# Four tiles in place of two in the first pass over h

## The chip, the cores and the metric

One core of a Trainium2 chip runs the whole kernel in one launch. The metric is the time of the device in microseconds (us), lower is better. Matrix products run on TensorE (PE in the profile), everything elementwise on VectorE (DVE) and ScalarE (ACT), a few small steps on GpSimd (POOL), and SyncE (SP) issues the loads of weights.

## The reference, cut to what matters

Two transformer blocks follow each other on a sequence of 256 tokens with 2048 channels, all in float32. The part of the first block that the change touches:

```python
h = rms_norm(x, mix_norm_g)
q, kv, gate_logits, conv_in = split(h @ w_in)     # conv_in: 2 x 1024 columns
conv = silu(layer_norm(causal_depthwise_conv(a * sigmoid(gate))))   # a, gate = halves of conv_in
attn = nsa_attention(q, kv, gates, ...)           # compressed, selected and window branches
x = x + concat([attn, conv]) @ w_out
h = rms_norm(x, ffn_norm_g)
u = causal_depthwise_conv(h @ w_up, 3 taps)       # 2 x 5632 columns
x = x + (silu(gate) * a) @ w_down                 # a, gate = halves of u
```

The second block (adaptive scales from `c`, latent attention, gated linear attention, a gated feed-forward) takes the result.

## The kernel before, in words

**Precision.** Every large product is made of three: both operands are split into a high part (float32r) and the rest, and high x high, rest x high and high x rest are added in PSUM. For the weights ScalarE rounds a chunk (`w_hi`, L1147) and VectorE subtracts (`w_lo`, L1623).

**Weights.** All weights come in one stream of 933 chunks of 128 x 1024, in an order written by `make_plan`: 737 to be split, 4 raw ones and 192 of `w_ada`, which VectorE multiplies with silu(c) and sums (L1605) in between, at a rate per split chunk that `ada_until` sets. SyncE loads up to seven chunks ahead into `raw`; a slot is free again when its rest is taken. ScalarE and VectorE split up to four ahead (`PART_SLOTS`); `lead(i)` is the third split chunk behind chunk i, and both engines split that far before they take the result of the tile that ends with chunk i.

**Tiles and groups.** A tile is 128 output columns of a projection, with the weights as the stationary operand: 16 steps k over the 2048 channels, two chunks. Its result is [128 columns, 256 tokens] in one PSUM bank. Up-projection tiles use `h_both`, high and rest of h side by side, 512 columns (L593, L594); the others take three matmuls of 256 columns (L596 to L598). A group is 512 output columns with h (or the mixed values) stationary, two banks, one for each 128 tokens (L603, L606). `tiles["of"]` is the rotation of banks that tiles go through, (4, 5, 2, 3), `tiles["turn"]` the place in it; groups name their two banks. The rotation is set anew at L875 (behind the attention), at L1013 and at L1092. `free[b]` is the semaphore that says when bank b has been read, and `fill(b)` waits for it before the first matmul of a tile or a group.

**h stages.** Four times (stages 0 to 3) a normed x in `wide` is turned by TensorE (two transposes per k, L671, banks 6, 7, 0, 1), rounded by ScalarE (`h_hi`, L1179) and its rest taken by VectorE (`h_lo`, L1677). `need(k)` in `h_need` turns up to three k ahead of the k that the matmuls take. Stages 0 and 1 come before the convolution's projections and before the first feed-forward; there the first pass is a pair of tiles by turns (`tile_pair`), so that each k feeds two tiles. `WITH_H` says at which k ScalarE and VectorE put a weight chunk between.

**Order behind it.** After the pair of stage 0: a small matmul of the table of position biases (L702), the other 14 convolution tiles, 4 tiles for the compression, its small layer, 8 query tiles, one of gates, 4 key tiles, the group `value` in banks 2 and 7, then the attention's 16 units with the convolution's output projection between their steps. The last key tile is read by ScalarE (L1250), behind the silus of the convolution (L1260); the first scores need it. After the pair of stage 1, for each half of the feed-forward: its up tiles (44 in all, 22 for the value and 22 for the gate, those of the pair among them in half 0), each joined by VectorE (L1910), then the down-projection in four groups of banks (0, 1), (2, 3), (0, 1), (2, 3), each added to x by VectorE (L1878). Then the second block begins: stage 2, `c_q` in banks (0, 1), `c_kv` in (2, 3), four `gla_q` and four `gla_k` tiles (read by ScalarE, L1406), with turned latents in banks 0 and 1 and 6 and 7 between them, and the group `gla_v` 0 in (0, 1).

Of the kernel before, what the change touches and what calls it, by code (L numbers as in the profile page):

```python
# [13 lines left out]
P = 128  # L14
T = 256
TT = T // P
D = 2048
KD = D // P
# [11 lines left out]
DFF = 5632  # L30
# [36 lines left out]
class Plan:  # L67
# [3 lines left out]
    def __init__(self):  # L71
        self.chunks = []
        self.kinds = []
        self.groups = {}
        self.pairs = {}
        self.ada = [(v, kt, half) for v in range(6) for kt in range(KD) for half in range(2)]
        self.rate = 0.0
        self.due = 0.0
        self.keep = 0
        self.on_pool = set()  # L80
        self.pool_rate = 0.0
        self.pool_due = 0.0
        self.open = False
# [29 lines left out]
    def project(self, key, mat, col, n, k0=0, nk=KD, order=None):  # L113
        self.groups[key] = [self.piece(mat, kt, col, n) for kt in order or range(k0, k0 + nk)]

    def project_pair(self, key, first, second, mat, cols, n):
        self.groups[key] = [self.piece(mat, kt, col, n) for kt in range(KD) for col in cols]
        self.pairs[first] = self.pairs[second] = key

    def raw(self, key, mat, pieces):  # L120
        self.groups[key] = []
# [11 lines left out]
            self.put_ada()  # L133


def make_plan():
    p = Plan()
    kv = HEADS * DH
    gates = kv + N_BRANCH * 512
    conv = gates + N_BRANCH * HEADS  # L140
    p.project_pair("conv_first", ("conv_a", 0), ("conv_g", 0), "w_in", (conv, conv + CONV_CH), P)
    for j in range(1, CONV_TILES):
        p.project(("conv_a", j), "w_in", conv + P * j, P)
        p.project(("conv_g", j), "w_in", conv + CONV_CH + P * j, P)
    for s in range(2):
        for j in range(2):
            p.project(("cmp", s, j), "w_in", kv + 256 * s + P * j, P)
    p.raw("cmp_w1", "cmp_w1", 2 * CMP_LEN * DH // CHUNK)
    for j in range(8):
        p.project(("query", j), "w_in", P * j, P)  # L150
    p.project("gates", "w_in", gates, N_BRANCH * HEADS)
    for br in (1, 2):
        for j in range(2):
            p.project(("key", br, j), "w_in", kv + 512 * br + P * j, P)
    p.project("value", "w_in_v", 0, 512)
    for n in range(4):
        p.project(("out_conv", n), "w_out", 512 * n, 512, KD // 2, KD // 2)
    for n in range(4):
        p.ada_until(2 * KD, 0.58 if n in (1, 2) else 0)
        p.project(("out_attn", n), "w_out", 512 * n, 512, 0, KD // 2)  # L160
    for half in range(2):
        if half == 0:
            p.project_pair("up_first", ("up_a", 0), ("up_g", 0), "w_up", (0, DFF), P)
        p.ada_until(2 * KD, 0.53)
        for j in range(FF_HALF * half or 1, FF_HALF * (half + 1)):
            p.project(("up_a", j), "w_up", P * j, P)
            p.project(("up_g", j), "w_up", DFF + P * j, P)
        p.ada_until(2 * KD, 0.76)
        for n in range(4):
            p.project(("down1", half, n), "w_down", 512 * n, 512, FF_HALF * half, FF_HALF)  # L170
    p.finish_ada()
    p.project("c_q", "w_in_2", 0, Q_RANK)
    p.project("c_kv", "w_in_2_kv", 0, KV_RANK + ROPE + GATE_RANK)
    at = Q_RANK + KV_RANK + ROPE
    for h in range(GLA_HEADS):
        p.project(("gla_q", h), "w_in_2", at + P * h, P)
    at += GLA_HEADS * GLA_K
    for h in range(GLA_HEADS):
        p.project(("gla_k", h), "w_in_2", at + P * h, P)
    at += GLA_HEADS * GLA_K  # L180
    for n in range(2):
        p.project(("gla_v", n), "w_in_2", at + 512 * n, 512)
    at += GLA_HEADS * GLA_V + GATE_RANK
    for n in range(2):
        p.project(("gla_r", n), "w_in_2", at + 512 * n, 512)
    p.project("q_rope", "w_uq_rope", 0, MLA_HEADS * ROPE, 0, Q_RANK // P)
    for h in range(MLA_HEADS):
        p.project(("q_nope", h), "w_uq_nope", P * h, P, 0, Q_RANK // P)
    for h in range(MLA_HEADS):
        p.project(("k_nope", h), "w_uk", P * h, P, 0, KV_RANK // P)  # L190
    for n in range(2):
        p.project(("mla_v", n), "w_uv", 512 * n, 512, 0, KV_RANK // P)
    for n in range(4):
        p.project(("out2", n), "w_out_2", 512 * n, 512, order=MIX_ORDER)
    p.open = False
    p.ada_until(0, 0.2)
    for half in range(2):
        for g, col, n in FF_GROUPS[half]:
            p.project(("gate", g), "w_ffn_gate", col, n)
            p.project(("up", g), "w_ffn_up", col, n)  # L200
        for n in range(4):
            p.project(("down2", half, n), "w_ffn_down", 512 * n, 512, FF_HALF * half, FF_HALF)
    return p
# [36 lines left out]
class Stream:  # L240


    def __init__(self, plan):
# [19 lines left out]
        for key, pieces in plan.groups.items():  # L263
# [8 lines left out]
                        self.used[i] = n  # L272
            self.done[key] = n
            self.final[key] = pieces[-1][0]
        for key, pair in plan.pairs.items():
            self.done[key], self.final[key] = self.done[pair], self.final[pair]


class Seen:
# [11 lines left out]
def two_blocks(nc, WEIGHTS, X, PARAMS, PARAMS1, PARAMS2, POSITIONS, COND, FINAL_ROW, OUT):  # L291
# [12 lines left out]
    with ctx:  # L304
# [163 lines left out]
        banks = [both[:, 0, :], both[:, 1, :]] + [ctx.enter_context(nc.psum_tensor(f"bank{b}", [P, 512], F32)) for b in range(2, 8)]  # L468
        bank_of = {}
        FIRST_CHUNKS = (0, groups["up_first"][0][0], c_first, gate_first)  # L470
        WITH_PAIR = {0: 0, 2: 1, 4: 2, 6: 3, 11: 4}
        WITH_GROUP = {k: k // 2 for k in range(0, KD, 2)}
        WITH_H = (WITH_PAIR, WITH_PAIR, WITH_GROUP, WITH_GROUP)
        TURN_BANKS = ((6, 7, 0, 1), (6, 7, 0, 1), (6, 7, 4, 5), (6, 7, 4, 5))
        LATENT_BANKS = (6, 7, 0, 1, 6, 7)
        WITH_GLA_Q = ((), (), (), (0, 1))
# [86 lines left out]
        def tensor_program(e):  # L563
# [121 lines left out]

                return need

            def tile_pair(key, first, second, a_hi, a_lo, need, free_first, free_second, a_both=None):
                both = (4, 5)
                tiles["turn"] += 2  # L690
                bank_of[first], bank_of[second] = both
                whole(project(key, P, both, [banks[b][:, 0:T] if a_both is None else banks[b][:, :] for b in both], a_hi, a_lo, need, True, by_turns=True, a_both=a_both))
                free[4], free[5] = free_first, free_second

            w.wait_ge(gains_landed, 16)
            need = h_need(0, lambda k: (h_ready, k + 1))
            tile_pair("conv_first", ("conv_a", 0), ("conv_g", 0), h_hi, h_lo, need, (conv_a_ready, 1), (conv_g_ready, 1))
            K1 = BUCKETS + 1
            w.wait_ge(params_landed, 16)
            w.wait_ge(params1_landed, 16)  # L700
            fill(7)
            e.matmul(banks[7][0:HEADS, 0:ROW], param1("rel_bias")[0:K1, :], param1("one_hot")[0:K1, :], start=True, stop=True).then_inc(table_made, 1)  # L702
            free[7] = table_ready, 1
            for j in range(1, CONV_TILES):
                tile(("conv_a", j), h_hi, h_lo, need, (conv_a_ready, j + 1))
                tile(("conv_g", j), h_hi, h_lo, need, (conv_g_ready, j + 1))
            for s in range(2):
# [171 lines left out]
                free[pair[0]], free[pair[1]] = (residual, 8 + 2 * n + 1), (residual, 8 + 2 * n + 2)  # L879

            need = h_need(1, lambda k: (h_ready, 16 + k + 1))
            tile_pair("up_first", ("up_a", 0), ("up_g", 0), h_hi, h_lo, need, (up_joined, 1), (up_joined, 2), h_both)
            for half in range(2):
                for j in range(FF_HALF * half or 1, FF_HALF * (half + 1)):
                    wide_tile(("up_a", j), need, (up_joined, 2 * j + 1))
                    wide_tile(("up_g", j), need, (up_joined, 2 * j + 2))
                ff_need = lambda k, half=half: w.wait_ge(ff_ready, FF_HALF * half + k + 1)
# [1743 lines left out]
```

## Time and profile before

| | us |
|---|---|
| three timed runs | 2235.58, 2238.95, 2239.26 |
| their median | 2238.95 |
| the profiled execution | 2235.5 |
| its span, first to last instruction | 2233.7 |
| TensorE busy | 2193.6 |
| VectorE busy | 1611.1 |
| ScalarE busy | 1119.3 |

A row of the timeline gives the start and the length of an instruction, or of a run of like ones (x8), and in square brackets the idle time ahead of it with what ended it. Matmuls overlap: one of 512 columns shows about 0.39 us, while the next starts 0.23 us after it, so the starts tell the pace and a short wait doesn't show as idle time. A row of the windows gives, for a stretch, its length, the busy time of each engine with the number of instructions, the granted TensorE clock as a share of the full one, the busy share of the DMA engines and GB/s.

### The profile page before, as it was taken

The numbers are of one execution on the slowest core, as the hardware profiler recorded it, in microseconds if no ns is written. First come the engines' busy times: TensorE is split into PE (matmuls) and PEld (weight loads), VectorE is DVE, ScalarE is ACT, GpSimd is POOL, SyncE is SP. The second block draws the span as 40 slices with busy tenths as digits, with TensorE's granted clock in tenths as the row PEclk, the third lists the DMA queues.
The fourth block names the chain that finished last, engine by engine and source line by source line (L and its number), as shares of the span: only waits on it lengthen the run. The fifth ranks groups of instructions, "written<-read, shape, count | busy, mean of one in ns | idle before, by whom it ended". The sixth has DMA issues, their size and how long they took to land.

```text
span 2233.7 us, 30478 instructions
## 1 busy us (share of the span) xinstructions
PE 2193.6 (98%) x12130; PEld 1883.6 (84%) x12130; DVE 1611.1 (72%) x2423; ACT 1119.3 (50%) x1670; POOL 29.6 (1%) x63
## 2 busy tenths in 40 slices
PE   7999999999999999999989999989999999999998
PEld 7999887888888888888879787878888888888986
DVE  6998885899998799998865655566555555544555
ACT  5434774555554455554454655555444444444343
POOL 1000000000000000000000000000000000000000
PEclk9999999999999999999999999999999999999999
DMA  8644436688889888889955551647666677655563
GB/s 271 217 162 142 153 97 209 221 294 285 291 301 369 320 281 289 291 287 361 341 157 185 179 179 57 225 134 250 226 228 224 227 230 232 217 188 190 187 211 120
DMA packets 138223, 504.13 MB, mean 226 GB/s; under 512 B 15616, under 2 KB 15760, under 8 KB 137184
## 3 DMA queue, kind: packets, MB, share of 16 engines
q1 hardware_dynamic: 136512, 494.42, 65.5%
q0 software_dynamic: 1280, 5.65, 1.0%
q8 instruction: 96, 1.57, 0.3%
q10 hardware_dynamic: 288, 2.10, 0.3%
q14 instruction: 47, 0.39, 0.0%
HBM read 499.61 MB, written 2.51 MB: 225 GB/s over the span
## 4 chain that ended last, share of the span: by engine, by line
PE 85%; DVE 11%; ACT 2%; issue 1%; DMA 0%; POOL 0%; SPq 0%; DVEq 0%; ACTq 0%; POOLq 0%
PE bank L603 20%; PE both L603 18%; PE bank L606 10%; PE both L606 9%; PE bank L593 7%; DVE w_lo L1623 5%; PE bank L594 4%; PE bank L596 4%; PE bank L598 4%; PE bank L597 4%; DVE raw L1605 2%; ACT ffn_a L1345 1%; ACT ffn_g L1351 1%; PE bank L830 1%; PE both L787 1%
## 5 line engine op out<-in xcount | busy, mean ns | idle before, releaser
L1623 DVE TENSOR_TENSOR w_lo<-raw,w_hi 128x1024 fp32r<-128x1024 f32 x737 | 893.8, 1221 | 450.1 <-ACT w_hi L1147 448.6
L1147 ACT ACTIVATE w_hi<-raw 128x1024 fp32r<-128x1024 f32 x737 | 767.9, 1054 | 640.9 <-PE bank L606 296.6
L593 PE MATMUL bank<-h_both,w_hi 128*128 128x512 f32 x1408 | 356.5, 394 | 1.8 <-DVE h_both L1677 1.8
L593 PEld LDWEIGHTS bank<-h_both,w_hi 128*128 128x128 f32 x1408 | 253.2, 189 | 47.0 <-DVE h_both L1677 2.5
L1605 DVE SCALAR_TENSOR_TENSOR raw<-raw,silu_c 128x1024 f32<-128x1024 f32 x192 | 233.9, 1218 | 0.0
L603 PE MATMUL bank<-w_hi,h_both 128*128 128x512 f32 (+2 forms) x1024 | 233.9, 372 | 0.0
L603 PE MATMUL both<-w_hi,h_both 128*128 128x512 f32 (+1 forms) x960 | 231.9, 383 | 1.7 <-DVE h_both L1697 1.7
L603 PEld LDWEIGHTS bank<-w_hi,h_both 128*128 128x128 f32 x1024 | 181.8, 188 | 33.1 <-issue 0.3
L594 PEld LDWEIGHTS bank<-h_both,w_lo 128*128 128x128 f32 x1408 | 192.1, 190 | 13.7
L603 PEld LDWEIGHTS both<-w_hi,h_both 128*128 128x128 f32 x960 | 171.3, 191 | 34.5 <-DVE h_both L1697 2.9
L594 PE MATMUL bank<-h_both,w_lo 128*128 128x256 f32 x1408 | 196.3, 282 | 0.0
L596 PE MATMUL bank<-h_both,w_hi 128*128 128x256 f32 (+1 forms) x656 | 165.1, 288 | 0.6 <-DVE h_both L1677 0.6
L597 PE MATMUL bank<-h_both,w_hi 128*128 128x256 f32 (+1 forms) x656 | 162.5, 284 | 0.0
L596 PEld LDWEIGHTS bank<-h_both,w_hi 128*128 128x128 f32 (+1 forms) x656 | 125.6, 191 | 2.2 <-DVE h_both L1677 1.1
L606 PE MATMUL bank<-w_lo,h_both 128*128 128x512 f32 (+2 forms) x512 | 126.4, 371 | 0.0
L597 PEld LDWEIGHTS bank<-h_both,w_hi 128*128 128x128 f32 (+1 forms) x656 | 125.7, 192 | 0.1
L606 PE MATMUL both<-w_lo,h_both 128*128 128x512 f32 (+1 forms) x480 | 121.5, 377 | 0.0
L603 PE MATMUL bank<-w_hi,ff_hi 128*128 128x512 f32 x352 | 111.0, 389 | 0.0
L603 PE MATMUL bank<-w_hi,ff_lo 128*128 128x512 f32 x352 | 111.0, 389 | 0.0
L603 PE MATMUL both<-w_hi,ff_hi 128*128 128x512 f32 x352 | 108.7, 390 | 0.6 <-ACT w_hi L1147 0.6
L603 PE MATMUL both<-w_hi,ff_lo 128*128 128x512 f32 x352 | 108.5, 389 | 0.0
L606 PEld LDWEIGHTS bank<-w_lo,h_both 128*128 128x128 f32 x512 | 91.4, 188 | 16.2
(366 smaller groups left out, 2624.4 us busy)
## 6 DMA issues: line engine op xcount, KB each, us to landing
raw<-weights SPq DMA_DIRECT2D x924, 512.0 KB, 4.5
raw<-weights SPq DMA_DIRECT2D x5, 504.0 KB, 4.2
x<-x SPq DMA_DIRECT2D x2, 1024.0 KB, 5.6
bias<-bias_rows POOLq DMA_DIRECT2D x8, 256.0 KB, 11.6
silu_c<-c ACTq DMA_DIRECT2D x2, 1024.0 KB, 4.6
gate_row<-gate_rows POOLq DMA_DIRECT2D x2, 1024.0 KB, 8.7
out<-x SPq DMA_DIRECT2D x8, 256.0 KB, 2.1
final_row<-final_row POOLq DMA_DIRECT2D x1, 1024.0 KB, 5.1
```

Source lines behind the costliest of these rows:

```text
L593: return e.matmul(out, hi, a_both[:, k, :, :].rearrange("p a t -> p (a t)"), start=first, stop=last)
L594: return e.matmul(out[:, 0:T], lo, a_hi[:, k, :], start=False, stop=False)
L596: e.matmul(out, hi, a_hi[:, k, :], start=opens and first, stop=False)
L597: return e.matmul(out, hi, a_lo[:, k, :], start=False, stop=False)
L598: return e.matmul(out, lo, a_hi[:, k, :], start=False, stop=closes and last)
L603: t = e.matmul(outs[o], stationary[:, k, o * P:(o + 1) * P], hi, start=opens and first and stationary is a_hi, stop=False)
L606: t = e.matmul(outs[o], a_hi[:, k, o * P:(o + 1) * P], lo, start=False, stop=closes and last)
L787: t = e.matmul(both[:, side, br * n:(br + 1) * n], queries[r, j, tt * P:(tt + 1) * P], keys[r, br, j // GQA, 0:n], start=True, stop=True)
L830: t = e.matmul(banks[b][DH * side:DH * side + DH, 0:P], values[:, sb, br, hk * DH:(hk + 1) * DH], weights_T[v % 2][:, (2 * side + br) * (t ...
L1147: e.activation(w_hi[:, n % PART_SLOTS, 0:widths[i]], raw[:, i % RAW_SLOTS, 0:widths[i]], ACT.Copy).then_inc(hi_ready, 1)
L1605: e.scalar_tensor_tensor(src, src, 1.0, silu_c[:, half, :], ALU.mult, ALU.mult, accum_out=ada_parts[:, v, kt, half:half + 1]).then_inc(ada ...
L1623: e.tensor_tensor(w_lo[:, slot, 0:widths[i]], raw[:, i % RAW_SLOTS, 0:widths[i]], w_hi[:, slot, 0:widths[i]].bitcast(F32), ALU.subtract).t ...
```

## The change

In stages 0 and 1 the first pass takes four tiles by turns, two of each half of the projection, in place of two. The plan orders their weights as k by k of four tiles, eight chunks; `WITH_H` has the same places in all four stages. `tile_four` puts them in banks 4, 5, 2 and 3 and sets the rotation of the tiles behind it to six banks.

```diff
-    def project_pair(self, key, first, second, mat, cols, n):
+    def project_four(self, key, tiles, mat, cols, n):
         self.groups[key] = [self.piece(mat, kt, col, n) for kt in range(KD) for col in cols]
-        self.pairs[first] = self.pairs[second] = key
+        for of in tiles:
+            self.fours[of] = key
...
+FIRST_CONV = [("conv_a", 0), ("conv_g", 0), ("conv_a", 1), ("conv_g", 1)]
+FIRST_UP = [("up_a", 0), ("up_g", 0), ("up_a", 1), ("up_g", 1)]
...
-    p.project_pair("conv_first", ("conv_a", 0), ("conv_g", 0), "w_in", (conv, conv + CONV_CH), P)
-    for j in range(1, CONV_TILES):
+    p.project_four("conv_first", FIRST_CONV, "w_in", (conv, conv + CONV_CH, conv + P, conv + CONV_CH + P), P)
+    for j in range(2, CONV_TILES):
...
-            p.project_pair("up_first", ("up_a", 0), ("up_g", 0), "w_up", (0, DFF), P)
+            p.project_four("up_first", FIRST_UP, "w_up", (0, DFF, P, DFF + P), P)
         p.ada_until(2 * KD, 0.53)
-        for j in range(FF_HALF * half or 1, FF_HALF * (half + 1)):
+        for j in range(FF_HALF * half or 2, FF_HALF * (half + 1)):
...
-        WITH_PAIR = {0: 0, 2: 1, 4: 2, 6: 3, 11: 4}
-        WITH_GROUP = {k: k // 2 for k in range(0, KD, 2)}
-        WITH_H = (WITH_PAIR, WITH_PAIR, WITH_GROUP, WITH_GROUP)
+        WITH_H = ({k: k // 2 for k in range(0, KD, 2)},) * 4
...
-            def tile_pair(key, first, second, a_hi, a_lo, need, free_first, free_second, a_both=None):
-                both = (4, 5)
-                tiles["turn"] += 2
-                bank_of[first], bank_of[second] = both
-                whole(project(key, P, both, ..., by_turns=True, a_both=a_both))
-                free[4], free[5] = free_first, free_second
+            def tile_four(key, members, a_hi, a_lo, need, frees, a_both=None):
+                tiles["of"], tiles["turn"] = (4, 5, 2, 3, 0, 1), 4
+                four = tiles["of"][0:4]
+                for of, b in zip(members, four):
+                    bank_of[of] = b
+                whole(project(key, P, four, ..., by_turns=True, a_both=a_both))
+                for b, free_at in zip(four, frees):
+                    free[b] = free_at
```

The loops on TensorE behind both calls start at j = 2 in place of 1. ScalarE's and VectorE's programs change only through the plan and `WITH_H`.

## Rows read from the trace of the kernel before

**Rows 1.** The profile's first part: busy us, share, instructions of each engine.

```profile
PE 2193.6 (98%) x12130; PEld 1883.6 (84%) x12130; DVE 1611.1 (72%) x2423; ACT 1119.3 (50%) x1670; POOL 29.6 (1%) x63
```

**Rows 2.** Waits of TensorE, for h: us in total, times, longest.

```profile
PE bank L593 <- DVE h_both L1677: 1.8, 2, 1.3
PE bank L596 <- DVE h_both L1677: 0.6, 1, 0.6
```

**Rows 3.** Timeline of TensorE in the h stages: start, length, what.

```profile
16.27 0.63 PE L671 MATMUL bank<-lasting,wide 128*128 128x128 f32 x2
16.68 0.58 PE L596 MATMUL bank<-h_both,w_hi 128*128 128x256 f32 x1
...
400.73 0.38 PE L671 MATMUL bank<-lasting,wide 128*128 128x128 f32 x2
401.61 0.73 PE L593 MATMUL bank<-h_both,w_hi 128*128 128x512 f32 x2 [0.49 <-DVE h_both L1677]
...
404.49 0.38 PE L671 MATMUL bank<-lasting,wide 128*128 128x128 f32 x2
404.62 0.71 PE L593 MATMUL bank<-h_both,w_hi 128*128 128x512 f32 x2
```

**Rows 4.** Windows of both pairs, and of the two tiles behind the second.

```profile
13.97:30.46 16.49, 16.49 (x121) 16.12 (x121) 14.27 (x36) 11.17 (x20) 0.00 (x0) 1.00 0.72 281
...
394.27:410.51 16.24, 15.74 (x88) 13.20 (x89) 13.66 (x26) 9.23 (x17) 0.00 (x0) 0.90 0.54 161
410.51:421.65 11.14, 11.14 (x65) 9.83 (x64) 9.73 (x16) 4.92 (x9) 0.00 (x0) 1.00 0.69 221
```

**Rows 5.** Timeline of TensorE where value begins, and the second unit's scores.

```profile
233.14 2.00 PE L603 MATMUL bank<-w_hi,h_both 128*128 128x512 f32 x8
...
242.48 1.13 PE L787 MATMUL both<-keys,queries 64*128 64x256 f32 x8
```

**Rows 6.** Timeline of ScalarE there: the last rounding and the key's copy.

```profile
236.84 1.04 ACT L1147 ACTIVATE w_hi<-raw 128x1024 fp32r<-128x1024 f32 x1
237.79 0.36 ACT L1250 ACTIVATE keys<-bank 128x256 f32<-128x256 f32 x1
```

**Rows 7.** Idle ahead of two h stages (timeline), and TensorE's windows with granted clock.

```profile
391.94 0.55 PE L671 MATMUL bank<-lasting,wide 128*128 128x128 f32 x3 [3.05 <-DVE wide L1637]
...
1135.69 1.75 PE L671 MATMUL bank<-lasting,wide 128*128 128x128 f32 x7 [4.18 <-DVE wide L1637]
...
394.00:396.00 2.00, 1.73 (x5) 0.50 0.54 106
396.00:398.00 2.00, 2.00 (x9) 0.66 0.72 211
...
1143.00:1145.00 2.00, 2.00 (x8) 0.53 1.08 35
...
217.00:219.00 2.00, 0.48 (x4) 1.00 0.00 0
```

**Rows 8.** Timelines where half 1 of the up-projection begins: TensorE, VectorE.

```profile
765.75 1.98 PE L593 MATMUL bank<-h_both,w_hi 128*128 128x512 f32 x8
...
765.95 1.29 DVE L1878 TENSOR_TENSOR x<-bank,x 128x512 f32<-128x512 f32 x2 [0.34 <-PE bank L606]
```

**Rows 9.** Timelines where gla_v begins: TensorE, ScalarE.

```profile
1228.78 1.09 PE L603 MATMUL both<-w_hi,h_both 128*128 128x512 f32 x4
...
1231.14 0.69 PE L942 MATMUL bank<-a_lr,phase 16*128 16x256 f32 x2 [0.81 <-DVE a_lr L2093]
...
1228.98 0.39 ACT L1406 ACTIVATE gla_k<-bank 128x256 f32<-128x256 f32 x1
```

**Rows 10.** Timelines behind the pairs: VectorE's join, ScalarE's rounding, VectorE's later wait.

```profile
413.91 0.42 DVE L1910 TENSOR_TENSOR up_a<-bank,up_low 128x256 f32<-128x256 f32 x1
...
416.88 1.99 ACT L1147 ACTIVATE w_hi<-raw 128x1024 fp32r<-128x1024 f32 x2
...
135.18 0.76 DVE L1766 TENSOR_TENSOR tokens<-bank,phase 128x256 f32<-128x256 f32 x2 [1.37 <-PE bank L598]
```

More of the change, by code:

```diff
@@ L74, in __init__ @@
         self.groups = {}
-        self.pairs = {}
+        self.fours = {}
         self.ada = [(v, kt, half) for v in range(6) for kt in range(KD) for half in range(2)]
@@ L274, in __init__ @@
             self.final[key] = pieces[-1][0]
-        for key, pair in plan.pairs.items():
-            self.done[key], self.final[key] = self.done[pair], self.final[pair]
+        for key, four in plan.fours.items():
+            self.done[key], self.final[key] = self.done[four], self.final[four]
 class Seen:
@@ L686, in h_need @@
                 return need
-            def tile_pair(key, first, second, a_hi, a_lo, need, free_first, free_second, a_both=None):
-                both = (4, 5)
-                tiles["turn"] += 2
-                bank_of[first], bank_of[second] = both
-                whole(project(key, P, both, [banks[b][:, 0:T] if a_both is None else banks[b][:, :] for b in both], a_hi, a_lo, need, True, by_turns=True, a_both=a_both))
-                free[4], free[5] = free_first, free_second
+            def tile_four(key, members, a_hi, a_lo, need, frees, a_both=None):
[3 more added lines that the diff above has]
+                    bank_of[of] = b
+                whole(project(key, P, four, [banks[b][:, 0:T] if a_both is None else banks[b][:, :] for b in four], a_hi, a_lo, need, True, by_turns=True, a_both=a_both))
+                for b, free_at in zip(four, frees):
+                    free[b] = free_at
             w.wait_ge(gains_landed, 16)
             need = h_need(0, lambda k: (h_ready, k + 1))
-            tile_pair("conv_first", ("conv_a", 0), ("conv_g", 0), h_hi, h_lo, need, (conv_a_ready, 1), (conv_g_ready, 1))
+            tile_four("conv_first", FIRST_CONV, h_hi, h_lo, need, [(conv_a_ready, 1), (conv_g_ready, 1), (conv_a_ready, 2), (conv_g_ready, 2)])
             K1 = BUCKETS + 1
@@ L703, in tensor_program @@
             free[7] = table_ready, 1
-            for j in range(1, CONV_TILES):
+            for j in range(2, CONV_TILES):
                 tile(("conv_a", j), h_hi, h_lo, need, (conv_a_ready, j + 1))
@@ L881, in tensor_program @@
             need = h_need(1, lambda k: (h_ready, 16 + k + 1))
-            tile_pair("up_first", ("up_a", 0), ("up_g", 0), h_hi, h_lo, need, (up_joined, 1), (up_joined, 2), h_both)
+            tile_four("up_first", FIRST_UP, h_hi, h_lo, need, [(up_joined, i + 1) for i in range(4)], h_both)
             for half in range(2):
-                for j in range(FF_HALF * half or 1, FF_HALF * (half + 1)):
+                for j in range(FF_HALF * half or 2, FF_HALF * (half + 1)):
                     wide_tile(("up_a", j), need, (up_joined, 2 * j + 1))
```

## The prediction

> **What bounds the kernel now.** I read the busy table first: TensorE is busy for 2193.6 of the span of 2233.7 us, VectorE for 1611.1, ScalarE for 1119.3 [rows 1]. So a change pays only where TensorE stands still. The list of TensorE's waits comes second, because the change is made to shorten waits for h: in the two stages that it touches TensorE waited for `h_both` for 1.8 + 0.6 us in all, three times [rows 2]. Then the timeline of TensorE through the second of these stages, for waits too short to be listed [rows 3], and a table of its busy time there [rows 4]. After that I left the stages and followed the banks, since the diff also changes which PSUM bank every later tile takes; what decides lies there [rows 5 to 9].
>
> **The h stages: what four tiles can win.** TensorE turns h (two transposes per k) and multiplies each k as soon as VectorE has its low half. With a pair a k brings 2 tiles of work, with four it brings 4; matmuls, transposes and weight chunks are the same in number, only earlier or later in the order. In the feed-forward stage a pair of transposes takes 0.13 us until the next matmul starts (404.49 to 404.62), but at 400.73 it is 0.88, so 0.75 too much [rows 3]. At the half clock such a pair takes 0.28 elsewhere and 0.41 at 16.27 to 16.68 us [rows 3], 0.13 too much; two more such places, one in each stage, hold 0.20 together. The first matmul's own waits (0.57 and 1.34 us) stay: they end with h's first low half, which four tiles don't bring sooner. With four, one k lasts about 1.2 us of TensorE and VectorE needs per two k two low halves (0.40 each, start to start) and one chunk's rest (1.22), 2.0 against 2.9 or more, so nothing is late there. Gain: 0.75 + 0.13 + 0.20 = 1.1 us. Its ends: nothing, if the waits only move; and, at the other end, all that the stages take beyond plain matmuls. The pair takes 16.24 us where the next two tiles take 11.14, 5.1 more, and the convolution's pair 16.49, where its 96 matmuls of 0.12 us would take 11.5, so 5.0 more [rows 4]. Most of this is 12 to 16 pairs of transposes and the half clock, which stay.
>
> **The burst behind four tiles.** Four tiles end at once, and ScalarE must open all four before it rounds the fourth chunk ahead. From the first join to the rounding that follows two tiles took 413.91 to 416.88, 3.0 us [rows 10]; the second two also carry a product, a silu and a rounding, so I estimate 3.4 to 4.4 us more, with about 0.5 to begin. The three chunks ready give TensorE 3 x 2.79 = 8.4 us (11.14 us for four chunks [rows 4]). The fourth is then rounded at 7.4 to 8.4: 0 to 0.3 us late. I take 0.2, with 0 and 3 as ends, because VectorE is nearly full there (9.73 of 11.14 us [rows 4]) and may not catch up. In the convolution VectorE starts its taps some 2 us later, since the sigmoid's table and four openings now come together. That lag has until VectorE's wait of 1.37 us at 135.18 us [rows 10] to vanish, and the short waits of 0.22 us per 11.5 us before it: cost 0. The table of position biases is made some 12 us later, but its rows are read by VectorE only after all taps, past 200 us: cost 0. Two chunks of the ada stream move from the first up-projection to the end of the second down-projection, where VectorE waits for ScalarE between two chunks: cost 0.
>
> **The banks: where it loses.** Before, tiles rotate over (4, 5, 2, 3), groups of two banks over (0, 1) and (2, 3). `tile_four` sets the rotation to (4, 5, 2, 3, 0, 1) at turn 4, and it stays so until it is set again. Counting turns gives the bank of each tile that a group of another kind follows.
>
> Place A, the end of the keys. Turns: 4 + 12 convolution tiles + 4 + 8 + 1 = 29 for key (1, 0), so key (2, 1) has turn 32, 32 mod 6 = 2, bank 2 (before: 32 mod 4 = 0, bank 4). `value` follows at once, in banks 2 and 7, and `fill(2)` now waits for `keys_ready` 4, ScalarE's copy of that key. In the trace value starts at 233.14 [rows 5], right behind the key's last matmul. ScalarE copies the key only at 237.79 to 238.15, behind eight silus of the convolution and two roundings, the last of them at 236.84, none of which wait for `value` [rows 6]. Before, two steps of value, 5.6 us, hide this. Now TensorE stands from 233.3 to 238.15: 4.9 us. Nothing behind it takes it back but a hidden wait of about 0.3 us at 242.48, where the second unit's scores wait for VectorE [rows 5]: of the lines of TensorE's waits none lies between 239 and 388 us, so there it is the bound. Net 4.6. Queued behind the waiting matmul are value's eight steps, all 16 attention units and the projections; ScalarE's rounding of chunks 73 and 74 waits in turn, with time to spare. Ends: 3.5, if ScalarE and VectorE had run ahead afterwards by more than I see, and 5.1.
>
> The clock at A. After the idle of 3.05 and 1.34 us the granted clock was 0.50 from 394 and rose inside 396:398 [rows 7]; after 4.18 + 1.42 us it was 0.50 from before 1137 until past 1143 [rows 7]. These are the two levels of 1.2 and 2.4 GHz. A stands 4.9 us in one piece, between the two, so I expect a fall. Half speed for 3.1 us costs 1.6 us, for some 6 us 3.0. I take 2.1, and 0 and 3.0 as ends: 0 because the shorter idle of 217:219 (busy 0.48 of 2.00 us) left the clock at 1.00 [rows 7].
>
> The Trainium skill (TensorE: Matmul & The Clock Gate, What's actually happening) says that the gate follows how busy TensorE has lately been, by a beat that doesn't start with the kernel, so that the length of the slow stretch differs between runs. By it the 2.1 us would scatter over the same ends; no row of one run can show that.
>
> Place B, from the first down-projection back to up tiles. Half 0 has 40 tiles in turns 4 to 43; up_a 22 has turn 44, 44 mod 6 = 2, bank 2 (before: bank 4). The last down group sits in (2, 3) and its residual must be added first. Its last matmul's slot ends at 765.75, VectorE starts the two additions at 765.95, 1.29 us for both, so the first ends near 766.64 [rows 8]: 0.9 us of wait, with 0.7 and 1.2 as ends (a rest or an ada sum a little late). The second bank is free by then. Half 1 ends with turns 86 and 87 in banks 2 and 3, but its first down group takes (0, 1), free long before.
>
> Place C, the second block. gla_k 3 has turn 95, bank 1, and gla_v 0 in (0, 1) waits for its copy, 1228.98 to 1229.37 instead of starting at 1228.78: 0.65 us. But six matmuls later TensorE already waits 0.81 us, until 1231.14, for VectorE's `a_lr`, whose chain doesn't hang on gla_v [rows 9]. So C costs 0; without that cover, 0.65.
>
> In the trace the rotation over four banks never makes a tile wait: both waits of tiles are for h [rows 2]. So two more banks bring nothing, and the rotation now meets the groups' banks. Against this reading stands the Trainium skill (Perfetto Trace Analysis, Matmul Optimizations), which advises to use all eight PSUM banks. By it six banks cost nothing and A and B fall out of the sum, which is then -0.9.
>
> **Sum.** -1.1 + 0.2 + 4.6 + 2.1 + 0.9 = +6.7 us. The profiled execution took 2235.5 (span 2233.7 and 1.8 around it), so 2242.2 by it. The runs shown spread from 2235.58 to 2239.26 with the median at 2238.95; the mean of the four times is 2237.3, and with 6.7 that is 2244. By the median it would be 2245.7.
>
> **Rivals.**
> 1. The stall at A leaves the clock at full: 4.6 in place of 6.7, so +4.6, 2242. For it: the idle lies between two steady stretches of matmuls, while both falls shown come behind idle cut by transposes. Against it: 3.05 + 1.34 us was enough.
> 2. The other side: the h stages are a chain of waits and not of work. If doubling the matmuls per k hid the transposes and the half clock too, the gain would be up to 5.1 + 5.0 = 10.1 and the sum 6.7 + 1.1 - 10.1 = -2.3, so 2235, not slower. It decides from a gain of 6.7 us on. For it: the excess is there [rows 4]. Against it: TensorE's busy time fills 16.49 of 16.49 and 15.74 of 16.24 us [rows 4].
> 3. The change costs nothing at the banks: -1.1 + 0.2 = -0.9, 2236. It holds only if ScalarE had the key's copy done when value starts; the trace has it 4.65 us later [rows 5, 6]. (The rule of the Trainium skill named at C, Matmul Optimizations in Perfetto Trace Analysis, would give this.)
> 4. The burst: VectorE's lag behind the four up tiles doesn't vanish in the half, or the convolution's lag reaches the queries, where VectorE already sets the pace. Some 3 us more: +9.5, 2247.
>
> **Chances.** Forecast 0.6, rival 1 0.12, rival 2 0.07, rival 3 0.07, rival 4 0.14. A measurement tells 0.2%, 4.5 us, from no change. The forecast lies 2.2 us beyond that, and with its ends 4 of 5 of it count as slower; half of rival 1, all of rival 4: 0.48 + 0.06 + 0.14, about 0.7 slower. Rivals 2 and 3 are mostly within 0.2%: 0.26 same, 0.04 faster. The range goes from 2239 (gain 2, clock 0, lower ends at A and B, from 2237.3) to 2249 (the median with rival 4).
>
> **What would show it.** At A: a wait of 4 to 5 us of the first L603 of `value` for ScalarE's `keys` (L1250), and a clock below 1 behind it. At B: a wait of near 0.9 us of the first `h_both` matmul of half 1 for VectorE's x (L1878). At C: a wait of near 0.6 us for `gla_k`, and the one for `a_lr` nearly gone. In the h stages the 0.49 us wait gone and no other in its place. The forecast is wrong if A shows no wait, if either h stage shrinks by more than 2 us, or if chunks in the up-projection come more than 2.8 us apart.

## The result and the profile after

The changed kernel takes 2246.32 us (median of 5 runs, 2244.95 to 2248.45), the kernel before 2238.87 (5 runs, 2235.58 to 2239.26). The ratio on record is 1.0046, interval 1.0036 to 1.0057, so 8 to 13 us slower. It isn't the ratio of these two medians, which is 1.0033 (7.5 us): of the five runs of the kernel before, three lie near 2239 us and two near 2236. In its later sets of 23 to 27 runs the median is 2235.70 to 2236.26, 10.1 to 10.6 us below 2246.32. The profiled execution of the changed kernel took 2244.95, its span is 2243.1.

The busy table hardly moves: TensorE is busy 2.3 us more [rows 1], the other engines do what they did.

```profile
PE 2195.9 (98%) x12130; PEld 1885.7 (84%) x12130; DVE 1611.6 (72%) x2423; ACT 1118.6 (50%) x1670; POOL 29.5 (1%) x63
```

The list of TensorE's waits (us in total, times, longest) has four lines that the kernel before did not have; its own tile waits were two, both for h [rows 2]. The line numbers of the kernel after are 3 to 5 higher (L603 is L606, L593 is L596, L1147 is L1152).

```profile
PE bank L606 <- ACT w_hi L1152: 4.9, 1, 4.9
...
PE both L606 <- ACT w_hi L1152: 1.5, 1, 1.5
...
PE bank L596 <- DVE h_both L1682: 1.3, 1, 1.3
PE bank L596 <- DVE x L1883: 0.9, 1, 0.9
PE both L596 <- ACT w_hi L1152: 0.8, 1, 0.8
...
PE both L606 <- ACT gla_k L1411: 0.6, 1, 0.6
```

**Place A.** TensorE's timeline where `value` begins (before: 233.14 [rows 5]), ScalarE's there (before: [rows 6]), and TensorE's windows with the granted clock.

```profile
238.45 2.05 PE L606 MATMUL bank<-w_hi,h_both 128*128 128x512 f32 x4 [4.94 <-ACT w_hi L1152]
```

```profile
237.04 1.04 ACT L1152 ACTIVATE w_hi<-raw 128x1024 fp32r<-128x1024 f32 x1
237.99 0.36 ACT L1255 ACTIVATE keys<-bank 128x256 f32<-128x256 f32 x1
```

```profile
236.00:238.00 2.00, 0.00 (x0) 0.94 0.22 35
238.00:240.00 2.00, 1.55 (x4) 0.50 0.60 227
240.00:242.00 2.00, 2.00 (x7) 0.50 0.79 205
242.00:244.00 2.00, 2.00 (x6) 0.50 0.14 57
244.00:246.00 2.00, 2.00 (x9) 0.85 0.00 0
```

The bracket names `w_hi` (L1152), but behind that rounding stands the key's copy, 237.99 to 238.35, and 0.10 us behind its end the matmul starts. This is the case in which a wait for several semaphores is put down to a wrong one; which it was is settled below (experiment 8) by moving the copy.

To see where the time goes I compare the start of the n-th matmul in both traces; the difference is called the offset, and its place is given in the time of the kernel before. It is +0.2 us at 174 us, +5.3 at value's first matmul, +8.2 at 236.3, where the slow clock has done its part, +8.1 at 242.5, and +7.9 at 391.9, where the second h stage begins. Inside an h stage the n-th matmul isn't the same one in both kernels, so there I read the offset ahead of the stage and behind the four tiles, at 421.7 us.

**The h stage and the burst.** The burst is what follows when four tiles end at once: ScalarE and VectorE have to take four results in a row. TensorE at the start of the four up tiles and behind them, and VectorE as they end:

```profile
402.19 2.07 PE L596 MATMUL bank<-h_both,w_hi 128*128 128x512 f32 x4 [1.34 <-DVE h_both L1682]
...
437.95 1.90 PE L596 MATMUL both<-h_both,w_hi 128*128 128x512 f32 x7 [0.79 <-ACT w_hi L1152]
```

```profile
427.59 1.22 DVE L1610 SCALAR_TENSOR_TENSOR raw<-raw,silu_c 128x1024 f32<-128x1024 f32 x1
428.73 0.08 DVE L1610 DVE_READ_ACCUMULATOR raw<-raw,silu_c 128x1 f32 x1
428.73 1.22 DVE L1628 TENSOR_TENSOR w_lo<-raw,w_hi 128x1024 fp32r<-128x1024 f32 x1
429.87 0.42 DVE L1915 TENSOR_TENSOR up_a<-bank,up_low 128x256 f32<-128x256 f32 x1
```

The wait of 0.49 us [rows 3] is gone, the first of 1.34 stays, and the offset falls to +7.0 behind the four tiles. Then it rises to +8.0 by 448 us and +8.3 at the end of the half: four results wait while VectorE still sums an ada chunk and makes a rest, the first join starts 1.2 us behind the first matmul of the next tile (428.64), and ScalarE rounds the fourth chunk only from 436.85 on. VectorE doesn't catch up in this half. Of its joins I compared every fourth from 432 to 632 us: they come 9.05 to 9.16 us later than before (one, at 588 us, 7.99), while TensorE's matmuls come 8.0 to 8.3 later. The last join of the half starts 5.33 us behind the start of the down group (653.44), before it was 4.42 (649.57 and 645.15). So the down group's wait of 0.62 us became 1.53, in TensorE's timeline of before and of after:

```profile
654.11 0.70 PE L603 MATMUL both<-w_hi,ff_hi 128*128 128x512 f32 x2 [0.62 <-ACT w_hi L1147]
```

```profile
663.31 0.70 PE L606 MATMUL both<-w_hi,ff_hi 128*128 128x512 f32 x2 [1.53 <-ACT w_hi L1152]
...
775.97 2.06 PE L596 MATMUL bank<-h_both,w_hi 128*128 128x512 f32 x8 [0.88 <-DVE x L1883]
...
1238.56 1.15 PE L606 MATMUL both<-w_hi,h_both 128*128 128x512 f32 x4 [0.56 <-ACT gla_k L1411]
```

**Places B and C** are the second and third row of that fence: B makes the offset 10.3 (+1.1, before [rows 8]), C adds 0.7 that is gone six matmuls later, for the wait for `a_lr` [rows 9] no longer shows. Half clock cost 1.2 us less in the third h stage and 0.4 more in the fourth than in the profiled execution of before; the end is +9.45.

### The profile page after: what moved, and what is told of

It reads as the page before. It is cut to its first block, busy times and chain, and to the rows that moved or that the text cites. A ratio compares the mean times of both kernels' runs of the same rounds, so it can differ in the third digit from the quotient of the medians.

```text
span 2243.1 us, 30488 instructions
## 1 busy us (share of the span) xinstructions
PE 2195.9 (98%) x12130; PEld 1885.7 (84%) x12130; DVE 1611.6 (72%) x2423; ACT 1118.6 (50%) x1670; POOL 29.5 (1%) x63
## 4 chain that ended last, share of the span: by engine, by line
PE 86%; DVE 10%; ACT 2%; issue 1%; DMA 0%; POOL 0%; SPq 0%; DVEq 0%; ACTq 0%; POOLq 0%
PE bank L606 20%; PE both L606 18%; PE bank L609 10%; PE both L609 9%; PE bank L596 5%; DVE w_lo L1628 4%; PE bank L597 3%; PE bank L599 3%; PE bank L601 3%; PE bank L600 2%; PE both L596 2%; DVE raw L1610 2%; PE both L599 1%; PE both L597 1%; PE both L601 1%; PE both L600 1%
## 5 line engine op out<-in xcount | busy, mean ns | idle before, releaser
L1152 ACT ACTIVATE w_hi<-raw 128x1024 fp32r<-128x1024 f32 x737 | 768.7, 1054 | 646.6 <-PE bank L609 305.0
L596 PE MATMUL bank<-h_both,w_hi 128*128 128x512 f32 x960 | 246.3, 395 | 2.2 <-DVE h_both L1682 1.3
L606 PE MATMUL bank<-w_hi,h_both 128*128 128x512 f32 (+2 forms) x1024 | 236.1, 374 | 4.9 <-ACT w_hi L1152 4.9
L606 PE MATMUL both<-w_hi,h_both 128*128 128x512 f32 (+1 forms) x960 | 231.7, 383 | 2.2 <-DVE h_both L1702 1.7
L606 PEld LDWEIGHTS bank<-w_hi,h_both 128*128 128x128 f32 x1024 | 183.4, 190 | 38.7 <-ACT w_hi L1152 5.1
L596 PEld LDWEIGHTS bank<-h_both,w_hi 128*128 128x128 f32 x960 | 173.8, 190 | 33.2 <-DVE h_both L1682 1.6
L606 PEld LDWEIGHTS both<-w_hi,h_both 128*128 128x128 f32 x960 | 171.2, 191 | 34.8 <-DVE h_both L1702 2.5
L597 PEld LDWEIGHTS bank<-h_both,w_lo 128*128 128x128 f32 x960 | 130.9, 190 | 9.4
L597 PE MATMUL bank<-h_both,w_lo 128*128 128x256 f32 x960 | 133.8, 282 | 0.0
L596 PE MATMUL both<-h_both,w_hi 128*128 128x512 f32 x448 | 114.6, 392 | 0.8 <-ACT w_hi L1152 0.8
L606 PE MATMUL bank<-w_hi,ff_hi 128*128 128x512 f32 x352 | 111.0, 389 | 0.0
L606 PE MATMUL bank<-w_hi,ff_lo 128*128 128x512 f32 x352 | 110.9, 389 | 0.0
L599 PE MATMUL bank<-h_both,w_hi 128*128 128x256 f32 x432 | 109.7, 290 | 0.6 <-DVE h_both L1682 0.6
L606 PE MATMUL both<-w_hi,ff_hi 128*128 128x512 f32 x352 | 108.7, 390 | 1.5 <-ACT w_hi L1152 1.5
L606 PE MATMUL both<-w_hi,ff_lo 128*128 128x512 f32 x352 | 108.4, 389 | 0.0
L600 PE MATMUL bank<-h_both,w_hi 128*128 128x256 f32 x432 | 107.7, 285 | 0.0
L609 PEld LDWEIGHTS both<-w_lo,h_both 128*128 128x128 f32 x480 | 86.9, 189 | 16.6
```

The source lines that it names most:

```text
L596: return e.matmul(out, hi, a_both[:, k, :, :].rearrange("p a t -> p (a t)"), start=first, stop=last)
L597: return e.matmul(out[:, 0:T], lo, a_hi[:, k, :], start=False, stop=False)
L599: e.matmul(out, hi, a_hi[:, k, :], start=opens and first, stop=False)
L600: return e.matmul(out, hi, a_lo[:, k, :], start=False, stop=False)
L606: t = e.matmul(outs[o], stationary[:, k, o * P:(o + 1) * P], hi, start=opens and first and stationary is a_hi, stop=False)
L609: t = e.matmul(outs[o], a_hi[:, k, o * P:(o + 1) * P], lo, start=False, stop=closes and last)
```

## The experiments

Each is told by its ratio to the kernel before, measured beside it, and by its offsets. The 13 profiled executions, one of each kernel in this document, differ by up to 3 us for the clock alone (last section), so stretches are compared, not ends.

**1. Four tiles, banks as before.** Behind the first two tiles that follow each four (they take banks 0 and 1), the rotation is set back:

```diff
                 tile(("conv_g", j), h_hi, h_lo, need, (conv_g_ready, j + 1))
+                if j == 2:
+                    tiles["of"], tiles["turn"] = (4, 5, 2, 3), 6
...
                     wide_tile(("up_g", j), need, (up_joined, 2 * j + 2))
+                    if j == 2:
+                        tiles["of"], tiles["turn"] = (4, 5, 2, 3), 6
```

> Four tiles as in the change, but from j = 3 on the tiles rotate over (4, 5, 2, 3) with the turn of the kernel before, in both stages, so every later bank is the old one. Theory (the six-bank rotation costs 4.9 us of waiting and 2.9 of half clock at value, 1.0 at half 1 of the up-projection; four tiles themselves win 1.2 in the feed-forward's h stage and lose 2.4 to the burst): no wait at value, none at the first up tile of half 1, span 2233.7 - 1.2 + 2.4 = about 2235, ratio to before 1.0005 (0.9995 to 1.0015). Rival (the loss is the four tiles' own, the bank waits only stand where ScalarE and VectorE would have stopped TensorE a little later): the two waits go and others of the same sum appear in the attention, ratio 1.003 to 1.005.

Measured: 2236.87 against 2236.26 us, ratio 1.0002 [0.9993, 1.0010]; repeated beside other kernels, 2236.55 against 2235.70, 1.0005 [0.9996, 1.0014]. Neither value nor half 1 waits, and the list of waits keeps the burst and the lag:

```profile
PE both L606 <- ACT w_hi L1156: 1.6, 1, 1.6
...
PE both L596 <- ACT w_hi L1156: 0.8, 1, 0.8
```

Nearly the whole loss, 9 to 10 of the 10 us, hangs on the rotation of the banks. The repeat was expected so:

> The kernel of four tiles with the four banks of before once more, beside the next two on one chip. Theory: ratio 1.000, +0.9 at the start of the first down group and +1.8 at the end, counted from the end of the attention's offset.

Counted from 392 us its offset is +1.9 at the first down group and +2.8 behind the lag, 1.0 and 1.0 above what I expected: half clock lasted longer in its h stage (until 402.6 us, in the kernel before until 397.4), and the offset rose by 0.5 in it in place of falling. The waits of 0.8 and of 1.5 to 1.6 us are there in both.

**2. Two tiles, six banks.** The other half of the change alone:

```diff
-            tiles = {"turn": 0, "of": (4, 5, 2, 3)}
+            tiles = {"turn": 0, "of": (4, 5, 2, 3, 0, 1)}
...
-            tiles["of"], tiles["turn"] = (4, 5, 2, 3), 0
+            tiles["of"], tiles["turn"] = (4, 5, 2, 3, 0, 1), 0
```

> Two tiles and the plan of the kernel before, only the rotation has six banks from the start of the kernel and again behind the attention. Turn 32 (the last key) is bank 2 and turn 44 (the first up tile of half 1) is bank 2, as in the change. Theory: idle of 4.9 us ahead of value, then half clock worth 2.9, 0.9 to 1.0 at half 1, 0.6 at gla_v taken back by the wait for a_lr: span 2233.7 + 7.8 + 1.0 = about 2242.5, ratio 1.0035 to 1.004; no longer wait than 0.7 at the first down group of half 0. Rival (the four tiles' own loss): ratio within 1.001.

Measured: ratio 1.0036 [1.0024, 1.0049]. Value waits 4.95 us, half clock follows (offset +2.8 more by 236.3 us), B waits 0.9, C 0.6. No burst: the offset is +9.83 at 416 and at 645 us, 2.1 of it from a fall of the clock at 200 us and a longer half clock in the h stage. The wait at the first down group is 0.85 us, a little above the 0.7 that I set as its limit. So the banks' price needs no fourth tile.

**3. The wait filled.** In the changed kernel 20 matmuls of 512 columns into bank 6, which nobody reads, stand ahead of `value`:

```diff
+            fill(6)
+            for _ in range(20):
+                e.matmul(banks[6][:, :], h_hi[:, 0, 0:P], h_both[:, 0, :, :].rearrange("p a t -> p (a t)"), start=True, stop=True)
             out_project(0)
```

> The change, with 20 matmuls of 512 columns whose result nobody reads put into free bank 6 ahead of value, 20 x 0.227 = 4.5 us of work in the 4.9 us in which TensorE waits. Theory (the half clock behind the wait is a cost of its own): value starts where it did, clock 1.00 all through 236 to 245, the two steps of value take 5.5 us in place of 8.5, the ratio to before falls by 2.9 us or 0.0013 against the change's, to 1.0025 to 1.0033. Rival (after the wait TensorE is held by ScalarE's roundings of chunks 72 to 74, so a faster clock wins nothing): value's first two steps are faster, but a wait for w_hi or for the exps of the first units appears and the ratio stays at 1.004 to 1.0045.

Measured: ratio 1.0029 [1.0017, 1.0040], against 1.0046 of the changed kernel: 3.8 us less, and the intervals overlap only at their ends. The clock stays at 1.00 from 236 on, and the time is not lost twice: the offset rises by 5.1 at value's first matmul, as unfilled, and by nothing behind it. (The profiled execution came there with +3.7 already, 3.0 of it from a fall of the clock at 200 us, of which below.)

```profile
236.00:240.00 4.00, 4.00 (x23) 1.00 0.00 0
240.00:244.00 4.00, 3.60 (x16) 1.00 0.48 140
```

**4 and 5. One stage each, old banks.** Four tiles only in the feed-forward, then only in the convolution.

> Four tiles in the feed-forward's stage alone, two in the convolution's, old banks from j = 3 on. Theory: -1.2 us in the h stage, +1.4 at the burst (wait of near 0.8 us for ScalarE's fourth chunk), and VectorE's lag kept to the end of half 0 (+0.9 at the first down group, 1.5 in place of 0.6): ratio 1.000 to 1.001, and the same time as e1 within 0.5 us, because the convolution's stage neither wins nor loses. Rival (the convolution's four tiles lose, by the late taps): e4 is faster than e1 by 1 us or more.

Measured: 1.0005 [0.9996, 1.0013]; offset +0.5 at 391.9, −0.1 at 421.7, +1.0 at 448, +1.3 at 645, +2.3 behind the down group's wait. The median is 2237.42, 0.55 above experiment 1, so not faster: what four tiles cost comes from this stage.

> Four tiles only in the first pass of the convolution, a pair in the first feed-forward, and the four banks of before from the third tile of the convolution on. Theory (stage 0 neither wins nor loses, since the first matmul waits for h's first low half in any case and VectorE catches up before the queries): offset against the kernel before within 0.3 us at 42, 173, 233 and 416 us, at most +0.6 between, end within 0.5, ratio 1.000. Rival (stage 0 brings what was forecast of it, 0.3 us, or the lag of the convolution's taps reaches the queries): -0.3 throughout, or +1 and more from 141 us on.

Measured: 0.9999 [0.9990, 1.0008]; offset +0.1 at the first matmul of the stage's tiles, −0.2 at 42.8 and −0.1 from 141 to 770 us (the end is −1.3, for half clock ended sooner in the third h stage). The rival of a lag that reaches the queries fell. The other isn't told from the theory: counted from the stage's first matmul the four tiles gained 0.2 us, near the forecast 0.3 and within what runs differ by.

The clock tells more of this stage than the ratio does. In experiments 1 and 2 TensorE's matmuls of 256 columns go from 0.21 us apart to 0.12 near 17 us, some 1.4 us sooner than in the kernel before. With four tiles (1) the offset then goes from +0.1 to −0.9; with a pair (2) it stays at +0.1, for behind the transposes at 20.55 us the next matmul starts only at 21.44. So in these two executions four tiles used an early full clock, and the pair waited it away.

**6. Place A alone.** The kernel before with one edit, which puts the last key into bank 2:

```diff
+                if at_key == 2:
+                    tiles["turn"] += 2
                 steps = tile_steps(("key", br, j), h_hi, h_lo, need)
```

> The kernel before, two tiles in the first passes and four banks in the rotation, with one line added: the turn of the rotation is moved on by 2 ahead of the last key tile, so that this tile takes bank 2 in place of 4. Theory (the bank of one tile makes the stall at the value group, and the stall makes the clock fall): TensorE stands 4.9 us ahead of the first matmul of value, the granted clock is near 0.5 behind it, and the offset against the kernel before goes from 0 to about +5.3 at value's first matmul and to about +8 from 242 us on, then stays: the whole is +8, ratio 1.0035. Rival (the clock fell in the changed kernel because of what the four tiles altered earlier, not because of this idle time): +4.6 to +5, ratio 1.002, clock 1.00 through 238 to 245. Second rival (something other than the bank holds value): no wait, ratio 1.000.

```profile
238.44 3.75 PE L603 MATMUL bank<-w_hi,h_both 128*128 128x512 f32 x8 [4.94 <-ACT w_hi L1149]
```

Measured: 1.0036 [1.0023, 1.0048], offset +0.2 at 174, +5.3 at value, +7.6 at 236, +7.5 at 242.5, +7.7 to 1140 us. One bank of one tile makes the stall of 4.9 us, and the clock falls with it, for 2.3 us here.

**7. The changed kernel without A.** The same edit in the changed kernel, where it puts the key into bank 0.

> The changed kernel with the same line: the turn moves on by 2 ahead of the last key tile, which then takes bank 0 in place of 2. Places B and C and the six banks stay. Theory: the wait at value and the slow clock behind it vanish (-7.9), the rest stays: offset against the kernel before about +0.2 until 392 us, -0.9 after the four up tiles, +1.4 at the first down group, +2.5 behind the wait for x at the start of half 1, and about +2 to +2.5 at the end, ratio 1.001. Rival (value is held by the key's copy in any bank, for instance by the scores' wait for it, or the pause comes somewhere later): the loss stays above +6, ratio 1.003 or more.

Measured: 1.0013 [1.0004, 1.0022], offset +0.3 through 233 and 242.5 us, −0.2 at 421.7, +1.1 at 645, +2.0 behind the down group's wait, +3.1 behind B. So 0.33% of the 0.46 is A.

**8. The copy sooner.** The changed kernel, with its banks; ScalarE copies the last key among the silus (the copy behind them is taken out, the roundings there stay):

```diff
                         if i == CONV_TILES // 2:
+                            w.wait_ge(multiplied, done_at["key", 2, 1])
+                            e.activation(keys[:, 1, 1, :], banks[bank_of["key", 2, 1]][:, 0:T], ACT.Copy).then_inc(keys_ready, 1)
                             round_until(stream.splits[rounded[0]])
```

> The changed kernel, with its banks, but ScalarE copies the last key behind the fourth of the convolution's eight silus and ahead of the rounding of a weight chunk there, in place of behind all eight and two roundings. Theory (the idle time at value is the queue on ScalarE ahead of that copy): the copy ends near 234.6, TensorE waits 1.2 to 1.5 us ahead of value in place of 4.9, and that is too short to bring the clock down: offset against the kernel before about +1.5 at value, no half speed behind it, end about +3, ratio 1.0015. Rival (the copy is late for another cause, such as the key's own matmuls or the table of the silu): wait above 4 us, ratio 1.004 or more. Second rival (any idle at this place brings the clock down): wait 1.3 but +4.5 behind it, end +6, ratio 1.0025.

```profile
233.84 0.36 ACT L1265 ACTIVATE keys<-bank 128x256 f32<-128x256 f32 x1
```

```profile
234.30 2.06 PE L606 MATMUL bank<-w_hi,h_both 128*128 128x512 f32 x8 [1.08 <-issue]
```

Measured: 1.0018 [1.0009, 1.0027]. The copy ends at 234.20, value starts 0.10 behind it, the same distance as in the changed kernel, and the clock stays at 1.00. This settles what A waited for: the copy, not `w_hi`: value starts while the next rounding (234.10, 1.05 us) still runs. A wait of 1.1 us leaves the clock alone. The end is +4.0 where I expected +3, for in this execution the offset rose by 0.3 in the second h stage in place of falling.

**9. The ada chunks out of the burst.** Experiment 1, and none of the ada stream's chunks among the eight behind the four tiles; 4 sums move from the first up half to later parts. The same with the kernel before:

```diff
-        p.ada_until(2 * KD, 0.53)
-        for j in range(FF_HALF * half or 2, FF_HALF * (half + 1)):
+        p.ada_until(2 * KD, 0.53 if half else 0)
+        for j in range(FF_HALF * half or 2, FF_HALF * (half + 1)):
+            if j == 4:
+                p.ada_until(2 * KD, 0.53)
...
-        p.ada_until(2 * KD, 0.76)
+        p.ada_until(2 * KD, 0.86)
```

> Four tiles, the four banks of before, and no chunk of the ada stream among the eight weight chunks of the four tiles behind the first four (up tiles 2 and 3): 4 of VectorE's 192 sums move from the first up half, where they fell into the burst, to the second up half and the down-projections. Theory (the wait behind the four tiles and VectorE's kept lag are made of sums of 1.14 us that stand between, while VectorE has no slack left in this half): TensorE's wait of 0.8 us for the fourth chunk vanishes, the last join of half 0 ends no later behind the start of the down group than in the kernel before (4.4 us, in place of 5.3), its wait there falls from 1.5 to 0.6 or less, and the gain of 0.9 to 1.2 us of the h stage stays: end 1.5 to 2.3 us below the kernel of four tiles with the old banks, 0 to 1 us below the kernel before, ratio 0.9997. Rival (the wait comes from ScalarE's and VectorE's order at the joins alone and the lag from the taps, not from the sums): both waits stay within 0.2 us, ratio 1.0005.

> The kernel before with the same change of the ada stream alone: none of its chunks among the eight behind the pair. What the four tiles themselves bring is then read against this kernel. Theory: the lag of VectorE in half 0 gets smaller by the 4 sums (4.6 us), so its wait of 0.6 us at the first down group vanishes: -0.6, end -0.5, ratio 0.9998. Rival (the sums moved into the down-projections cost there what they saved): ratio 1.000 to 1.0005, with new waits in the down groups.

Measured: with four tiles 2234.23 us against 2235.70, ratio 0.9993 [0.9985, 1.0002]; in the kernel before 2235.95, ratio 0.9999 [0.9990, 1.0007]. In the former TensorE waits 0.19 us in place of 0.79 for the fourth chunk, VectorE takes up the first join at once,

```profile
421.77 0.42 DVE L1921 TENSOR_TENSOR up_a<-bank,up_low 128x256 f32<-128x256 f32 x1 [0.84 <-ACT up_low L1337]
```

```profile
429.86 1.88 PE L598 MATMUL both<-h_both,w_hi 128*128 128x512 f32 x7 [0.19 <-ACT w_hi L1158]
```

and its last join of the half starts 3.34 us behind the down group (648.40 and 645.06), with no wait there at all. The offset is +0.1 at 391.9, −0.5 at 421.7, −0.1 at 645, −1.0 at 656. In the latter it is +3.7 at the first three places and +2.8 at 656: the down group's wait goes there too (−0.9). So of the 1.0 us from 391.9 to 656 some 0.9 belong to the sums, not to the four tiles, whose gain of 0.6 and burst of 0.4 leave little. The four-tile kernel is 2.3 us below its own repeat of experiment 1 in the same set; below the kernel before it is by 1.5 us, which the interval doesn't tell from nothing.

## Why the prediction was right or wrong

**Right.** What bounds the kernel, the direction, A's place and releaser, B and C. The main term was A at 4.9 idle: 4.94. B at 0.9: 0.88 idle, +1.1 in the offset. C at 0: +0.7, then taken back. The 0.3 us that a hidden wait was to take back behind A are there as well: the offset falls from +8.2 at 236.3 to +8.1 at 242.48 and +7.9 at 300, and by 0.3 in experiments 2, 6 and 8 too. The measured 2246.3 lies in the range.

**Wrong: the size.** Forecast +6.7, measured 0.46% or 10.3 us by the ratio, +9.4 in the profiled executions. That the forecast time, 2244, is only 2.3 us off is partly luck: it starts from 2237.3, the mean of four times, 1.0 to 1.6 us above the later medians of the kernel before. Term by term, from the offsets:

| step of the prediction | forecast | measured |
|---|---|---|
| the h stages: what four tiles can win | −1.1 | 0 and −1.0 |
| the burst behind four tiles | +0.2 | +1.3, and +0.9 at the down group |
| place A, the stall, less what is taken back | +4.6 | +4.8 |
| the clock at A | +2.1 | +2.9 |
| place B | +0.9 | +1.1 |
| place C | 0 | 0 |
| what differs by run: the start, the clock of stages 2 and 3 | none | +0.2 and −0.8 |
| sum | +6.7 | +9.4 |

**The step that failed is "the burst behind four tiles".** Its mechanism was named, but as a term of the sum it was far too small: +0.2 forecast, +1.3 and +0.9 measured, which is 2.0 of the 2.7 us missed. Two things in it were off.

First, when the fourth chunk is ready. From the first join to the rounding behind the openings the trace has 7.0 us (429.87 to 436.85), inside the 6.4 to 7.4 that the prediction's parts give. But VectorE, which works three chunks ahead, still owed an ada sum and a rest and began at 1.2 us, not at 0.5; and TensorE waits for the end of that rounding, 1.04 us more. The parts alone give 7.9 to 8.9 us with it, not the 7.4 to 8.4 that stand there. It took 9.3 us (428.64 to 437.95), and the three chunks ready lasted 8.5: 0.79 us of wait.

Second, the lag. The prediction had 9.73 of 11.14 us busy [rows 4] in hand, and still put the lag's price inside the 0.2; I set it beside the forecast as rival 4, with 0.14. In this half VectorE didn't take back the 0.9 us (the joins above), and they came due at the down group, where the wait went from 0.62 to 1.53 us. Experiments 1, 4 and the repeat show both waits with old banks (0.8 and 1.5 to 1.6 us), experiment 9 that they go with the sums.

**Smaller misses.** The clock at A cost 2.9 us in the changed kernel, 2.8 in experiment 2 and 2.3 in experiment 6; 2.1 lies below all three, and within its ends. What differs is how much of the half clock lay behind value's first matmul: 6.1, 5.9 and 4.9 us. The Trainium skill (TensorE: Matmul & The Clock Gate, What's actually happening) lets the slow stretch differ by run; these three agree with it. One k of four tiles takes 1.4 us of matmuls by [rows 4] (11.14 us for 32 k of a tile, times four), not 1.2; the 2.9 for two k beside it is right. And the clock of 1.00 in [rows 4] for the convolution's pair is not what the pace shows: matmuls of 256 columns start 0.21 us apart until 18.3 us and 0.12 behind it.

In stage 1, from 391.9 to 421.7 us, the gain depends on where the half clock lies. The offset falls by 1.0 in the changed kernel, by 0.8 in experiment 3 and by 0.5 to 0.6 in experiments 4, 7 and 9. Where half clock reaches further into the stage it rises, by 0.3 to 0.5 with four (experiments 1, its repeat, 8) and by 0.3 to 0.6 with a pair (6, 2): the gain then hardly shows.

**The rivals.** 1, the clock stays: fell, 0.50 for 6 us. 2, the h stages as a chain of waits: fell, 1.0 of up to 10.1 us in the changed kernel; the stages' excess is transposes and half clock, as the busy rows said. 3, banks are free: fell, and experiment 2 shows the reverse by itself, +0.36%. That is also what this case says of the rule of the Trainium skill (Perfetto Trace Analysis, Matmul Optimizations) to use all eight banks: more banks in the tiles' rotation brought nothing where no tile waited for one, and cost 8 us where the rotation met a group. 4, the lag: right in kind, and its +9.5 lies beside the measured +9.4, but partly by luck, for the burst and the lag came to 2.0 us more than forecast and not 3, and the clock at A added 0.8.

## What to carry to other kernels

A rotation of buffers is part of the schedule: when it grows, count, at each place where another user takes a fixed buffer, who had it last and where its reader stands in its own queue. The reader's queue, not its work, was the price here (a copy of 0.36 us behind silus and roundings). Where several results now end at once, ask what the engine that takes them still owes from working ahead, and if it has no slack, carry the lag to the next place where the order forces it to be level.

## What the runs showed of the hardware

The clock fell without idle time. In 4 of 13 profiled executions (experiments 2, 3, the repeat of 1, and the kernel before with ada later) it fell near 201 us, where TensorE was busy in every window, and stayed at 1.00 there in the other 9. What ran just before is a series of 32 matmuls of 30 columns (the scores of the compressed tokens, L750 before), 3.6 us long; that they are the cause is not shown. TensorE's windows of the kernel before and of the kernel before with ada later:

```profile
196.00:200.00 4.00, 4.00 (x38) 1.00 0.45 152
200.00:204.00 4.00, 4.00 (x35) 1.00 0.43 135
204.00:208.00 4.00, 4.00 (x31) 1.00 0.46 131
```

```profile
196.00:200.00 4.00, 4.00 (x38) 1.00 0.61 204
200.00:204.00 4.00, 4.00 (x24) 0.61 0.48 139
204.00:208.00 4.00, 4.00 (x22) 0.53 0.45 131
```

Such a fall costs 1.5 to 3.0 us of offset. The timed runs of the kernel before lie in part near 2236 and in part near 2239 us. A fall of this size would explain that, and the mean granted clock on record is 0.992 in the runs near 2239 and 0.992 to 0.995 in those near 2236; but timed runs leave no trace, so it stays open. A stall of 4.9 us brought the clock down in each of the three profiled executions that had it. One of 1.1 us (experiment 8) did not, nor one of 0.4 (experiment 3), nor those of 1.53 and 0.88 us in the changed kernel. The prediction's reading that a short idle leaves the clock alone, and a long one between steady stretches doesn't, holds for these.
